# Adding a projection's output bias to the residual on GpSimd instead of as four matrix products

## The chip, the cores and the metric

The kernel runs on one core of one Trainium2 chip, as one program. The metric is the device time in microseconds (us) of one execution; of several runs the median counts, and lower is better. The core has five engines that run side by side, each with its own instruction stream: TensorE (PE in the rows, with PEld for its weight loads), VectorE (DVE), ScalarE (ACT), GpSimd (POOL) and SyncE (SP), which starts the weight transfers. They meet only at semaphores.

## The reference: what is computed

Two transformer-like blocks over 256 tokens of width 1024, in float32. The first block has a banded attention, a squared-ReLU MLP, a Griffin recurrent layer and a second MLP; the second block has a gated MLP, a mixing layer and another gated MLP. The change is about the last line of the recurrent layer and the residual that it is added to:

```python
def rglru_block(h, w_in, b_in, conv_w, conv_b, w_ga, b_ga, w_gx, b_gx, a_param, w_o, b_o):
    u = jnp.einsum('bsd,de->bse', h, w_in) + b_in
    ...            # convolution over 4 taps, two sigmoid gates, a scan over time
    out = hs.astype(h.dtype) * y_br
    return jnp.einsum('bse,ed->bsd', out, w_o) + b_o
...
        h = h + mix                       # mix is the rglru_block of rmsnorm(h)
        h = h + sq_relu_mlp(rmsnorm(h, norm_mlp[layer]), mlp_w1[layer], mlp_w2[layer])
```

`b_o` has 1024 numbers, one for each column of `h`, and is the same for all 256 tokens.

## The kernel before, in words

The residual `h` stays in SBUF as two tiles of 128 tokens by 1024 columns. All order is written by hand: each engine has one function (`sync`, `scalar`, `vector`, `gpsimd`, `tensor`) that issues its instructions in program order, and waits on semaphores where it needs another engine.

Every weight matrix comes in pieces of 128x2048 float32 (1 MB). A piece is split into two float32r parts, since one float32r product alone would be too coarse: ScalarE copies `raw` to `w_hi` (`hi(n)`, L386), VectorE writes `w_lo = raw - w_hi` (`lo(n)`, L784), and TensorE makes three products for each block (high by high, high by low, low by high). Pieces of 8 row blocks go through `u_piece` (`u_block`, L1456 to L1459), pieces of output projections through `d_piece` and `d_part` (L1493).

At each layer's start (`turn(j, ...)` on three engines) VectorE adds the accumulators to `h` (L805), TensorE transposes `h` (L1519), ScalarE and VectorE split it to `xT_hi` and `xT_lo` (L400, L813). The norm's row factors follow later and beside: VectorE makes `var` (L820), GpSimd raises it to the power -1/2 (`rstds(j)`, L1385), VectorE scales the identity by it (`diags(j)`, L828, two of 128x128), TensorE multiplies these with ones (`spread(j)`, L1561), and VectorE copies the result to `rms` (L851).

The recurrent layer is called L1 (`N_REC` is its first piece, `N_RO` the first piece of its output projection). TensorE goes through eight `u_piece`s. Between their blocks stand `spread(L1)` (in the second piece) and the small products `gates(n)` (L1764, L1765, from the third piece on). `gates(n)` waits for three convolution taps of VectorE (`conv(p)`, L1165), which need `x_pair(p)` (L1156), which needs `rms`. On VectorE the order after `var` is: `lo(N_REC + 2)`, the two `diags`, a small fill of the convolution's padding (L1199), `lo(N_REC + 3)`, the copy of `rms`, `x_pair(0)`, `conv(0)`. GpSimd has `rstds(L1)`, then four products `bx` (L1417) and four `squares` (L1423), all 128x512.

The bias: GpSimd's queue starts a transfer that lays `b_o` over all 128 partitions. During the first MLP ScalarE and VectorE split it into a high and a low part, one in even and one in odd rows (L595, L596, L1136 to L1145). Before the output projection, TensorE writes the bias into the four accumulators with four products that contract over two rows only (L1786), in four different row groups of the array; the projection's products add to that. The first of them, in `d_piece(N_RO)`, waits for `z_lo` (L1196), which VectorE finishes late.

Of the kernel before, what the change touches and what calls it, by code (L numbers as in the profile page):

```python
# [7 lines left out]
F32R = mybir.dt.float32r  # L8
BF16 = mybir.dt.bfloat16
ACT = mybir.ActivationFunctionType  # L10
ALU = mybir.AluOpType
# [94 lines left out]
def r32(ap):  # L106
    return ap.bitcast(F32)


def build(nc, A, out):  # L110
    def sb(name, shape, dt=F32):
        return nc.alloc_sbuf_tensor(name, shape, dt)[tuple(slice(None) for _ in shape)]
# [22 lines left out]
    tiny = sb("tiny", [P, 6, 4])  # L135
    sink = sb("sink", [P, HEADS_2])
    vbuf = sb("v", [P, T, D])
    b_o = sb("b_o", [P, D], F32R)
    both = sb("both", [P, P], F32R)
    firsts = sb("firsts", [P, 2])  # L140
    work_bytes = 47 * 1024
    work = nc.alloc_sbuf_tensor("work", [P, work_bytes // 4], F32)
    bank = [nc.alloc_psum_tensor(f"bank{i}", [P, 512], F32)[:, :] for i in range(8)]
# [2 lines left out]
    def at(kib, *shape):  # L146
        n, o = int(np.prod(shape)), int(kib * 256)
        assert (o + n) * 4 <= work_bytes, (kib, shape)
        v = work[:, o:o + n]
        if len(shape) == 1:  # L150
            return v
        names = "abcd"[:len(shape)]
        return v.rearrange(f"p ({' '.join(names)}) -> p {' '.join(names)}", **dict(zip(names, shape)))
# [8 lines left out]
    def vec(name, i=0):  # L162
# [42 lines left out]
        "bx_done"))  # L205
    a_done, sq_done, m_done, mult_done, b_done, hs_done, y_done, o_done = (sem(n) for n in (
        "a_done", "sq_done", "m_done", "mult_done", "b_done", "hs_done", "y_done", "o_done"))
    bo_hi, bo_rest, bo_done = sem("bo_hi"), sem("bo_rest"), sem("bo_done")

    mix_left, pc_closed, pc_left, pool_d, d_left, k_rot, v_turned, v2_done = (sem(n) for n in (  # L210
        "mix_left", "pc_closed", "pc_left", "pool_d", "d_left", "k_rot", "v_turned", "v2_done"))
# [67 lines left out]
            return pair(z_hi[:, p, :]), pair(z_lo[:, p, :])  # L279
        return blocks(xT_hi, p), blocks(xT_lo, p)  # L280

    bo_raw, bo_low = at(24, D), at(28, D)
    nf = at(8, D)

    q2, k2, v2 = at(24, 4, S), at(28, 4, S), vbuf[:, :, 0:P]
# [61 lines left out]
    def row_bcast(a, n, rows=P):  # L347
        return bass.AP(tensor=a.tensor, offset=a.offset, ap=[[0, rows], [1, n]])
# [32 lines left out]
    def scalar(e):  # L381
# [66 lines left out]
                e.wait_ge(hn_done, t + 1)  # L448
                e.activation(at(16 + 4 * t, D), h[:, t, :], ACT.Square, accum_out=ssq2[:, t:t + 1]).then_inc(hn_ss, 1)

        def feed_forward(f, beside=None):
            if f.nu == 2:
                low_leaves(f, 0, 0)
            if f.j != M1:
                hi(f.n0 + LOOK)
            if f.nu == 2:
                if f.j == F1:
                    normed_squares()
                low_leaves(f, 0, 1)
                hi(f.n0 + 1 + LOOK)  # L460
                gate(f, 0)
            z_finish(f, 0)
            if f.j == M1:
                hi(f.n0 + LOOK)
            for p in range(1, f.pairs):
                n = f.ups(p)
                if beside and p == 6:
                    beside()
                if n + LOOK < TOTAL:
                    hi(n + LOOK)  # L470
                if f.nu == 2:
                    gate(f, p)
                    if n + 1 + LOOK < TOTAL:
                        hi(n + 1 + LOOK)
                z_finish(f, p)
                if n + f.nu + LOOK < TOTAL:
                    hi(n + f.nu + LOOK)
# [112 lines left out]
        hi(N_WO + 2 + LOOK)  # L590
        split_o(a1, 3)

        def bias_hi():
            e.wait_ge(in_b_o, 16)
            e.activation(b_o, bo_raw, ACT.Copy).then_inc(bo_hi, 1)  # L595
            e.activation(both, ones[:, 0:P], ACT.Copy).then_inc(bo_hi, 1)  # L596

        turn(M0, N_WO + 3 + LOOK)
        feed_forward(FM0, bias_hi)


        turn(L1, N_REC - 1 + LOOK)
# [178 lines left out]
    def vector(e):  # L781
# [122 lines left out]
            e.wait_ge(hn_done, 2)  # L904
            e.tensor_tensor(rstd, rstd, rstd2, ALU.mult).then_inc(rstd_both, 1)

        def feed_forward(f, beside=None):
            if f.nu == 2:
                sums(f, 0, 0, tmp[0])
                if f.j == F1:  # L910
                    normed_h()
            if f.j != M1:
                lo(f.n0 + LOOK)
            if f.nu == 2:
                if f.j == F1:
                    normed_variance()
                sums(f, 0, 1, tmp[1])
                lo(f.n0 + 1 + LOOK)
                if f.j == F1:
                    both_rstds()  # L920
                    diags(F1)
            if f.nu == 1:

                e.wait_ge(var_done, f.j + 1)
                e.reciprocal(down_scale, var).then_inc(scale_done, 1)
            else:
                spread(f.j)
                e.tensor_scalar(down_scale, rstd, 0.5, None, ALU.mult).then_inc(scale_done, 1)
                gate(f, 0)
            z_finish(f, 0)  # L930
            if f.j == M1:
                lo(f.n0 + LOOK)
            for p in range(1, f.pairs):
                n = f.ups(p)
                if beside and p == 7:
                    beside()
                if n + LOOK < TOTAL:
                    lo(n + LOOK)
                if f.nu == 2:
                    gate(f, p)  # L940
                    if n + 1 + LOOK < TOTAL:
                        lo(n + 1 + LOOK)
                z_finish(f, p)
                if n + f.nu + LOOK < TOTAL and not (f.j == F1 and p == f.pairs - 1):
                    lo(n + f.nu + LOOK)
# [99 lines left out]
        def beside(a, j, first_waits=()):  # L1045

            if j > 1:
                copy_turned(a, j - 1)
            for hd in range(2):
                mask_and_max(a, j, hd)  # L1050
# [80 lines left out]
        split_o(a1, 3)  # L1131
        lo(N_WO + 2 + LOOK)

        def bias_split():

            e.tensor_tensor(firsts, ident[:, 0:2], ident[:, 32:34], ALU.add).then_inc(bo_rest, 1)  # L1136
            for i in (2, 3):
                e.wait_ge(bo_rest, i - 1)
                e.tensor_tensor(firsts, firsts, ident[:, 32 * i:32 * i + 2], ALU.add).then_inc(bo_rest, 1)
            e.wait_ge(bo_hi, 1)  # L1140
            e.tensor_tensor(bo_low, bo_raw, r32(b_o), ALU.subtract).then_inc(bo_rest, 1)
            e.wait_ge(bo_rest, 4)
            e.tensor_scalar(bo_low, bo_low, firsts[:, 1:2], None, ALU.mult).then_inc(bo_rest, 1)
            e.wait_ge(bo_rest, 5)
            e.scalar_tensor_tensor(out=b_o, in0=r32(b_o), scalar=firsts[:, 0:1], in1=bo_low, op0=ALU.mult,  # L1145
                                   op1=ALU.add).then_inc(bo_done, 1)

        turn(M0, FM0.n0)
        feed_forward(FM0, bias_split)


        turn(L1, N_REC)
# [94 lines left out]
        mixed_lo(3)  # L1247
        lo(FM1.n0)

        turn(M1, FM1.n0, 1)  # L1250
        lo(FM1.n0 + 2)
        feed_forward(FM1)
# [129 lines left out]
    def gpsimd(e):  # L1382
# [24 lines left out]
        e.dma_start(gate_w[:, 1], A["w_gx"].rearrange("n c e -> c n e")).then_inc(in_gate_x, 16)  # L1407
        e.dma_start(pool_w, A["pool_w"].rearrange("n c e -> c n e")).then_inc(in_pool_w, 16)
        e.dma_start(sink, row_bcast(A["sink"], HEADS_2)).then_inc(in_sink, 16)
        e.dma_start(bo_raw, row_bcast(A["b_o"], D)).then_inc(in_b_o, 16)  # L1410


        rstds(L1)

        def bx(p):
            e.wait_ge(ig_done, 2 * p + 2)
# [28 lines left out]
    def tensor(e):  # L1445
# [331 lines left out]
        u_piece(N_REC + 6, bank[7])  # L1777
        e.wait_ge(x_left, 4)
        u_piece(N_REC + 7, bank[4])
        e.wait_ge(bo_done, 1)  # L1780
        e.wait_ge(bo_hi, 2)
        e.wait_ge(ig_done, KB)
        for t in range(T):
            for half in range(2):
                r = slice(32 * (2 * t + half), 32 * (2 * t + half) + 2)
                e.matmul(acc[t][half], both[r, :], b_o[r, half * HALF:(half + 1) * HALF], start=True, stop=False,  # L1786
                         skip_group_check=True)
        for i in range(2):
            e.wait_ge(mix_lo, 4 + i + 1)
            d_piece(N_RO + i, from_z(i))  # L1790
        one, two = (N_RO + 2, from_z(2)), (N_RO + 3, from_xT(3))
        e.wait_ge(mix_lo, 4 + 3)
        split(N_RO + 2)
# [209 lines left out]
```

## Time and profile before

| | us |
|---|---|
| three runs | 1012.96, 1013.86, 1013.97 |
| median | 1013.86 |
| profiled execution, its own time | 1013.26 |
| its span, first to last instruction | 1011.5 |
| TensorE busy | 1003.2 (99%) |
| VectorE busy | 684.5 (68%) |
| ScalarE busy | 556.8 (55%) |
| GpSimd busy | 35.0 (3%) |

A row of the timeline gives the start in us from the span's start, the duration in us, the engine, the line of the kernel, the operation, its output and inputs, and in brackets how long the engine sat idle before it and who ended that. Records of two instructions in a row on one engine overlap by some hundredths of a us, since an instruction is started before the one ahead of it has fully drained.

### The profile page before, as it was taken

To read this page: it belongs to the slowest core of one execution; us is meant where nothing else is said; L and a number is where in the kernel's file an instruction comes from. 1 tells how busy PE (TensorE), PEld (TensorE's weight loads), DVE (VectorE), ACT (ScalarE), POOL (GpSimd) and SP (SyncE) were. 2 spreads that over 40 slices of the span, in tenths; PEclk is the share of its full clock that TensorE was granted. 3 is DMA by queue.
4 is the path that set the end of the run, shared out by engine and by line. 5 is a ranking of instruction groups with operands and counts; after the bars stand their busy time and mean duration, and the time that the engine had idled before them with its cause. 6 is when DMAs were issued, how large, how long until landed. Compare 5 with 4: busy or idle time off the path is not lost.

```text
span 1011.5 us, 14177 instructions
## 1 busy us (share of the span) xinstructions
PE 1003.2 (99%) x5632; PEld 857.4 (85%) x5632; DVE 684.5 (68%) x925; ACT 556.8 (55%) x807; POOL 35.0 (3%) x38
## 2 busy tenths in 40 slices
PE   9999999999999999999999999999999999999997
PEld 7988788888889988888888888888888788888886
DVE  6777676666667887666566766656578767666564
ACT  6678654444456866443444645545457655545453
POOL 1000010000002300000000200000010010000000
PEclk9999999999999999999999999999999999999999
DMA  9943385564553445745655566565633365665621
GB/s 339 324 133 126 125 280 176 200 208 167 188 187 126 167 167 193 245 167 199 212 173 171 207 198 226 190 208 167 208 114 107 115 204 172 228 208 167 208 84 42
DMA packets 122287, 185.13 MB, mean 183 GB/s; under 512 B 3130, under 2 KB 100590, under 8 KB 122094
## 3 DMA queue, kind: packets, MB, share of 16 engines
q1 hardware_dynamic: 119952, 176.70, 52.4%
q0 software_dynamic: 1808, 6.93, 1.9%
q8 instruction: 45, 0.74, 0.3%
q10 hardware_dynamic: 462, 0.60, 0.2%
q14 instruction: 20, 0.16, 0.0%
HBM read 183.14 MB, written 1.07 MB: 182 GB/s over the span
## 4 chain that ended last, share of the span: by engine, by line
PE 96%; DVE 2%; ACT 1%; DMA 1%; issue 1%; SPq 0%
PE bank L1493 37%; PE bank L1470 28%; PE bank L1472 14%; PE bank L1456 3%; PE bank L1458 3%; PE bank L1459 3%; PE bank L1519 1%; DVE w_lo L784 1%; PE bank L1614 1%; PE bank L1665 1%; PE bank L1642 1%; PE bank L1626 1%; DMA raw<-in_w_qkv 1%; PE bank L1810 0%; PE bank L1811 0%
## 5 line engine op out<-in xcount | busy, mean ns | idle before, releaser
L784 DVE TENSOR_TENSOR w_lo<-raw,w_hi 128x2048 fp32r<-128x2048 f32 x164 | 374.0, 2289 | 130.5 <-ACT w_hi L386 130.5
L1470 PE MATMUL bank<-xT,w_hi 128*128 128x512 f32 x1216 | 431.4, 398 | 0.0
L1472 PE MATMUL bank<-xT,w_lo 128*128 128x256 f32 x1216 | 341.1, 280 | 0.0
L386 ACT ACTIVATE w_hi<-raw 128x2048 fp32r<-128x2048 f32 x164 | 311.7, 1908 | 37.5 <-PE bank L1493 33.5
L1470 PEld LDWEIGHTS bank<-xT,w_hi 128*128 128x128 f32 x1216 | 228.4, 188 | 55.7 <-issue 0.3
L1472 PEld LDWEIGHTS bank<-xT,w_lo 128*128 128x128 f32 x1216 | 229.6, 189 | 1.9
L1493 PE MATMUL bank<-w_hi,z_hi 128*128 128x512 f32 x472 | 153.9, 394 | 0.2
L1493 PE MATMUL bank<-w_lo,z_hi 128*128 128x512 f32 x472 | 152.3, 391 | 0.0
L1493 PE MATMUL bank<-w_hi,z_lo 128*128 128x512 f32 x472 | 151.7, 390 | 0.0
L429 ACT ACTIVATE work<-bank 128x256 f32<-128x256 f32 x152 | 49.8, 379 | 178.8 <-PE bank L1472 178.8
L859 DVE TENSOR_TENSOR work<-bank,work 128x256 f32<-128x256 f32 x152 | 57.1, 418 | 74.0 <-ACT work L429 74.0
L1493 PEld LDWEIGHTS bank<-w_lo,z_hi 128*128 128x128 f32 x472 | 88.6, 188 | 19.3 <-issue 0.2
L1493 PEld LDWEIGHTS bank<-w_hi,z_lo 128*128 128x128 f32 x472 | 88.6, 188 | 19.3
L1493 PEld LDWEIGHTS bank<-w_hi,z_hi 128*128 128x128 f32 x472 | 85.0, 188 | 18.5 <-issue 1.3
L1456 PE MATMUL bank<-xT,w_hi 128*128 128x256 f32 x304 | 89.9, 296 | 0.0
L444 ACT ACTIVATE z_hi<-work 128x512 fp32r<-128x512 f32 x54 | 34.1, 632 | 99.7 <-DVE work L876 53.0
L1458 PE MATMUL bank<-xT,w_hi 128*128 128x256 f32 x304 | 85.9, 282 | 0.0
L1459 PE MATMUL bank<-xT,w_lo 128*128 128x256 f32 x304 | 85.8, 282 | 0.0
L887 DVE TENSOR_TENSOR z_lo<-work,z_hi 128x512 fp32r<-128x512 f32 x54 | 37.4, 692 | 37.7 <-ACT z_hi L444 37.7
L1456 PEld LDWEIGHTS bank<-xT,w_hi 128*128 128x128 f32 x304 | 58.0, 191 | 2.4 <-issue 1.2
L1458 PEld LDWEIGHTS bank<-xT,w_hi 128*128 128x128 f32 x304 | 58.1, 191 | 0.3
L1459 PEld LDWEIGHTS bank<-xT,w_lo 128*128 128x128 f32 x304 | 58.1, 191 | 0.0
(215 smaller groups left out, 775.5 us busy)
## 6 DMA issues: line engine op xcount, KB each, us to landing
raw<-in_w SPq DMA_DIRECT2D x64, 1024.0 KB, 5.3
raw<-in_f_gate SPq DMA_DIRECT2D x22, 1024.0 KB, 5.3
raw<-in_f_up SPq DMA_DIRECT2D x22, 1024.0 KB, 5.8
raw<-in_f_down SPq DMA_DIRECT2D x22, 1024.0 KB, 4.9
raw<-in_w_in SPq DMA_DIRECT2D x13, 1024.0 KB, 5.4
raw<-in_w_qkv SPq DMA_DIRECT2D x9, 1024.0 KB, 8.6
raw<-in_w_o SPq DMA_DIRECT2D x4, 1024.0 KB, 5.0
raw<-in_rec_w_o SPq DMA_DIRECT2D x4, 1024.0 KB, 5.2
```

What stands on the lines that cost most here:

```text
L386: e.activation(w_hi[n % RING], raw[n % RAW], ACT.Copy).then_inc(hi_done, 1)
L429: e.activation(low[:, b * S:(b + 1) * S], bank[n][:, S:2 * S], ACT.Copy).then_inc(z_low, 1)
L444: e.activation(z_hi[:, s, :], tmp[f.nu], ACT.Copy).then_inc(zhi_done, 1)
L784: e.tensor_tensor(w_lo[n % RING], raw[n % RAW], r32(w_hi[n % RING]), ALU.subtract).then_inc(lo_done, 1)
L859: e.tensor_tensor(t[:, here], bank[n][:, 0:S], low[:, here], ALU.add).then_inc(z_sum, 1)
L887: e.tensor_tensor(z_lo[:, s, :], z, r32(z_hi[:, s, :]), ALU.subtract).then_inc(zlo_done, 1)
L1456: e.matmul(o, whi[:, k, cut], xT_hi[:, k, :], start=(k == 0 and b == 0), stop=False, skip_group_check=True)
L1458: e.matmul(o, whi[:, k, cut], xT_lo[:, k, :], start=False, stop=False, skip_group_check=True)
L1459: last = e.matmul(o, wlo[:, k, cut], xT_hi[:, k, :], start=False, stop=(k == KB - 1), skip_group_check=True)
L1470: e.matmul(bank[i], whi[:, k, cut], xT[:, k, :, :].rearrange("p b s -> p (b s)"), start=(k == 0), stop=False, skip_group_check=True)
L1472: last = e.matmul(bank[i][:, 0:S], wlo[:, k, cut], xT_hi[:, k, :], start=False, stop=(k == KB - 1), skip_group_check=True)
L1493: mm = e.matmul(acc[t][half], x, w[:, kk, half * 512:(half + 1) * 512], start=(first and kk == 0 and x is xhi and w is whi), stop=(last an ...
```

## The change

The four products are gone, and so is all that prepared them: ScalarE's two copies and VectorE's six instructions in the first MLP, and the tiles `both` and `firsts`. `b_o` is now plain float32, loaded by the same transfer. GpSimd adds it to the two tiles of `h`, with two instructions of 128x1024, straight behind `rstds(L1)`, once TensorE has transposed `h` for this layer. VectorE waits for both additions before it next adds to `h` (`turn(M1, ...)`). The first product of the output projection now starts its accumulators (`first`) in place of the bias products.

```diff
-    b_o = sb("b_o", [P, D], F32R)
-    both = sb("both", [P, P], F32R)
-    firsts = sb("firsts", [P, 2])
+    b_o = sb("b_o", [P, D])
...
-        def bias_hi():
-            e.wait_ge(in_b_o, 16)
-            e.activation(b_o, bo_raw, ACT.Copy).then_inc(bo_hi, 1)
-            e.activation(both, ones[:, 0:P], ACT.Copy).then_inc(bo_hi, 1)
...
-        def bias_split():
...
-            e.wait_ge(bo_hi, 1)
-            e.tensor_tensor(bo_low, bo_raw, r32(b_o), ALU.subtract).then_inc(bo_rest, 1)
...
+        e.wait_ge(bo_done, T)
         turn(M1, FM1.n0, 1)
...
         rstds(L1)
+
+        e.wait_ge(in_b_o, 16)
+        e.wait_ge(turned, KB * L1 + KB)
+        for t in range(T):
+            e.tensor_tensor(h[:, t, :], h[:, t, :], b_o, ALU.add).then_inc(bo_done, 1)
...
-        e.wait_ge(bo_done, 1)
-        e.wait_ge(bo_hi, 2)
         e.wait_ge(ig_done, KB)
-        for t in range(T):
-            for half in range(2):
-                r = slice(32 * (2 * t + half), 32 * (2 * t + half) + 2)
-                e.matmul(acc[t][half], both[r, :], b_o[r, half * HALF:(half + 1) * HALF], start=True, stop=False,
-                         skip_group_check=True)
         for i in range(2):
             e.wait_ge(mix_lo, 4 + i + 1)
-            d_piece(N_RO + i, from_z(i))
+            d_piece(N_RO + i, from_z(i), first=(i == 0))
```

GpSimd's queue in the changed program, from the last small transfer of the first MLP to the recurrent layer's squares (line numbers are those of the changed kernel; `work` holds `xc`, `ig`, `rr` and others):

```order
L1384 DMA sink<-in_sink 128x8
L1385 DMA b_o<-in_b_o 128x1024
L1360 TENSOR_TENSOR rstd<-var,minus_half 128x2 [waits var_done]
L1393 TENSOR_TENSOR h<-h,b_o 128x1024 [waits turned,in_b_o]
L1393 TENSOR_TENSOR h<-h,b_o 128x1024
L1397 TENSOR_TENSOR work<-work 128x512 [waits ig_done] x4
L1403 TENSOR_TENSOR work<-work 128x512 [waits a_done] x2
```

Before, the four `bx` stood right behind `rstd`; now the two additions stand between them.

TensorE's queue before, at the border from the last `u_piece` to the output projection:

```order
L1458 MATMUL bank<-xT,w_hi 128x256
L1459 MATMUL bank<-xT,w_lo 128x256
L1786 MATMUL bank<-b_o,both 128x512 [waits ig_done,bo_hi,bo_done]
L1786 MATMUL bank<-b_o,both 128x512 x3
L1493 MATMUL bank<-w_hi,z_hi 128x512 [waits lo_done,hi_done,mix_lo]
L1493 MATMUL bank<-w_hi,z_hi 128x512
```

The same place in the changed program:

```order
L1438 MATMUL bank<-xT,w_hi 128x256
L1439 MATMUL bank<-xT,w_lo 128x256
L1473 MATMUL bank<-w_hi,z_hi 128x512 [waits hi_done,lo_done,mix_lo,ig_done]
L1473 MATMUL bank<-w_hi,z_hi 128x512
L1473 MATMUL bank<-w_lo,z_hi 128x512 x2
```

The projection's first product now follows the last `u_piece` directly and takes over the wait for `ig_done`.

## Rows read from the trace of the kernel before

**Rows 1.** The page, parts 1, 2 and 4: busy time, granted clock, ending chain.

```profile
PE 1003.2 (99%) x5632; PEld 857.4 (85%) x5632; DVE 684.5 (68%) x925; ACT 556.8 (55%) x807; POOL 35.0 (3%) x38
...
PEclk9999999999999999999999999999999999999999
...
PE 96%; DVE 2%; ACT 1%; DMA 1%; issue 1%; SPq 0%
```

**Rows 2.** Waits of TensorE's products: engine, line, releaser, total us, times, longest.

```profile
PE bank L1650 <- POOL zeros L1387: 1.0, 1, 1.0
PE bank L1626 <- DVE work L990: 0.9, 2, 0.5
PE bank L1665 <- ACT w_hi L391: 0.2, 1, 0.2
```

**Rows 3.** Timeline, VectorE and GpSimd, at the start of the recurrent layer.

```profile
306.22 2.28 DVE L784 TENSOR_TENSOR w_lo<-raw,w_hi 128x2048 fp32r<-128x2048 f32 x1
306.40 2.69 POOL L1385 TENSOR_TENSOR rstd<-var,minus_half 128x2 f32<-128x2 f32 x1 [175.31 <-DVE var L820]
...
309.12 0.28 DVE L828 TENSOR_SCALAR diag<-ident,rstd 128x128 f32<-128x128 f32 x1 [0.61 <-POOL rstd L1385]
309.32 0.28 DVE L828 TENSOR_SCALAR diag<-ident,rstd 128x128 f32<-128x128 f32 x1
309.60 2.28 DVE L784 TENSOR_TENSOR w_lo<-raw,w_hi 128x2048 fp32r<-128x2048 f32 x1
312.17 0.42 DVE L851 COPY rms<-bank 128x256 f32<-128x256 f32 x1 [0.29 <-PE bank L1561]
...
314.05 0.48 DVE L1165 SCALAR_TENSOR_TENSOR work<-work,cols 128x256 f32<-128x256 f32 x1 [0.73 <-ACT work L619]
315.09 0.48 DVE L1165 SCALAR_TENSOR_TENSOR work<-work,cols 128x256 f32<-128x256 f32 x1
```

**Rows 4.** Timeline, TensorE's weight loads of `spread(L1)` and of `gates(0)`.

```profile
311.40 0.19 PEld L1561 LDWEIGHTS bank<-diag,ones 128*128 128x128 f32 x1
...
316.16 0.19 PEld L1764 LDWEIGHTS bank<-work,gate_w 128*128 128x128 f32 x1
```

**Rows 5.** Timeline, GpSimd's `bx` beside VectorE.

```profile
321.22 2.28 DVE L784 TENSOR_TENSOR w_lo<-raw,w_hi 128x2048 fp32r<-128x2048 f32 x1
322.16 2.50 POOL L1417 TENSOR_TENSOR work<-work 128x512 f32<-128x512 f32 x1 [13.07 <-ACT work L610]
...
325.12 1.30 POOL L1417 TENSOR_TENSOR work<-work 128x512 f32<-128x512 f32 x1 [0.47 <-ACT work L610]
325.97 0.74 DVE L1165 SCALAR_TENSOR_TENSOR work<-work,cols 128x256 f32<-128x256 f32 x1 [1.86 <-ACT work L619]
```

**Rows 6.** Timeline, GpSimd's `squares` beside VectorE.

```profile
344.46 1.04 POOL L1423 TENSOR_TENSOR work<-work 128x512 f32<-128x512 f32 x1 [2.26 <-ACT work L625]
345.46 1.04 POOL L1423 TENSOR_TENSOR work<-work 128x512 f32<-128x512 f32 x1
345.54 1.51 DVE L1176 SCALAR_TENSOR_TENSOR work<-work 128x512 f32<-128x512 f32 x1 [1.05 <-POOL work L1423]
346.97 0.68 DVE L1176 SCALAR_TENSOR_TENSOR work<-work 128x512 f32<-128x512 f32 x1
```

**Rows 7.** One tile's or line's instructions: duration in ns, min/median/max.

```profile
L784 DVE TENSOR_TENSOR w_lo<-raw,w_hi x164: 2272/2292/2295, 19.6 to 985.6; 128x2048 fp32r<-128x2048 f32 x164
...
L1141 DVE TENSOR_TENSOR work<-work,b_o x1: 1220/1220/1220, 197.5 to 197.5; 128x1024 f32<-128x1024 f32 x1
...
L1143 DVE TENSOR_SCALAR work<-work,firsts x1: 754/754/754, 198.7 to 198.7; 128x1024 f32<-128x1024 f32 x1
```

**Rows 8.** Timeline, the border before the output projection.

```profile
355.78 0.69 DVE L1196 TENSOR_TENSOR z_lo<-work,z_hi 128x512 fp32r<-128x512 f32 x1
...
356.07 0.28 PE L1459 MATMUL bank<-xT,w_lo 128*128 128x256 f32 x1
356.27 0.51 PE L1786 MATMUL bank<-b_o,both 2*128 2x512 f32 x4
356.71 0.73 PE L1493 MATMUL bank<-w_hi,z_hi 128*128 128x512 f32 x2
357.28 0.63 PE L1493 MATMUL bank<-w_lo,z_hi 128*128 128x512 f32 x2
```

**Rows 9.** Timeline, TensorE, a like border in the first MLP.

```profile
190.02 0.28 PE L1472 MATMUL bank<-xT,w_lo 128*128 128x256 f32 x1
190.13 0.63 PE L1493 MATMUL bank<-w_hi,z_hi 128*128 128x512 f32 x2
190.60 0.62 PE L1493 MATMUL bank<-w_lo,z_hi 128*128 128x512 f32 x2
```

More of the change, by code:

```diff
@@ L207, in build @@
         "a_done", "sq_done", "m_done", "mult_done", "b_done", "hs_done", "y_done", "o_done"))
-    bo_hi, bo_rest, bo_done = sem("bo_hi"), sem("bo_rest"), sem("bo_done")
+    bo_done = sem("bo_done")
     mix_left, pc_closed, pc_left, pool_d, d_left, k_rot, v_turned, v2_done = (sem(n) for n in (
@@ L280, in rec_home @@
         return blocks(xT_hi, p), blocks(xT_lo, p)
-    bo_raw, bo_low = at(24, D), at(28, D)
     nf = at(8, D)
@@ L449, in normed_squares, with feed_forward @@
                 e.activation(at(16 + 4 * t, D), h[:, t, :], ACT.Square, accum_out=ssq2[:, t:t + 1]).then_inc(hn_ss, 1)
-        def feed_forward(f, beside=None):
+        def feed_forward(f):
             if f.nu == 2:
@@ L466, in feed_forward @@
                 n = f.ups(p)
-                if beside and p == 6:
-                    beside()
                 if n + LOOK < TOTAL:
@@ L591, in scalar @@
         split_o(a1, 3)
-        def bias_hi():
-            e.wait_ge(in_b_o, 16)
-            e.activation(b_o, bo_raw, ACT.Copy).then_inc(bo_hi, 1)
-            e.activation(both, ones[:, 0:P], ACT.Copy).then_inc(bo_hi, 1)
         turn(M0, N_WO + 3 + LOOK)
-        feed_forward(FM0, bias_hi)
+        feed_forward(FM0)
         turn(L1, N_REC - 1 + LOOK)
@@ L905, in both_rstds, with feed_forward @@
             e.tensor_tensor(rstd, rstd, rstd2, ALU.mult).then_inc(rstd_both, 1)
-        def feed_forward(f, beside=None):
+        def feed_forward(f):
             if f.nu == 2:
@@ L934, in feed_forward @@
                 n = f.ups(p)
-                if beside and p == 7:
-                    beside()
                 if n + LOOK < TOTAL:
@@ L1132, in vector @@
         lo(N_WO + 2 + LOOK)
-        def bias_split():
[L1136 to L1139, printed above, removed]
-            e.wait_ge(bo_hi, 1)
-            e.tensor_tensor(bo_low, bo_raw, r32(b_o), ALU.subtract).then_inc(bo_rest, 1)
[L1142 to L1146, printed above, removed]
         turn(M0, FM0.n0)
-        feed_forward(FM0, bias_split)
+        feed_forward(FM0)
         turn(L1, N_REC)
@@ L1409, in gpsimd @@
         e.dma_start(sink, row_bcast(A["sink"], HEADS_2)).then_inc(in_sink, 16)
-        e.dma_start(bo_raw, row_bcast(A["b_o"], D)).then_inc(in_b_o, 16)
+        e.dma_start(b_o, row_bcast(A["b_o"], D)).then_inc(in_b_o, 16)
         rstds(L1)
+        e.wait_ge(in_b_o, 16)
+        e.wait_ge(turned, KB * L1 + KB)
+        for t in range(T):
+            e.tensor_tensor(h[:, t, :], h[:, t, :], b_o, ALU.add).then_inc(bo_done, 1)
         def bx(p):
```

## The prediction

> **What bounds the kernel now.** I read the page first: TensorE is busy for 1003.2 of 1011.5 us, and the chain that ended last lies on it for 96% [rows 1]. Then the waits: in the whole program TensorE's products wait for another engine only four times by name, 2.1 us together, the longest 1.0 [rows 2]. So there is one bound, TensorE, from end to end. Two things follow. Work taken from another engine is worth nothing. And work put on another engine costs nothing until it makes TensorE wait; from there on it costs all of it, because nothing behind gives it back. The question is thus how much slack TensorE's suppliers have where the additions now stand. The timeline of that place is [rows 3, 4].
>
> **What is taken away.** ScalarE's two copies and VectorE's six instructions in the first MLP (the two widest shown, 1.22 and 0.75 us, in [rows 7]) lie beside a TensorE that waits for neither: 0 us. The DMA of the bias is the same one as before.
>
> The four products start together at 356.27, in four row groups, and the projection's first product starts at 356.71 [rows 8]. At the like border in the first MLP the next product starts 0.11 us behind the last one of the piece (190.02 to 190.13) and the second pair 0.47 us behind the first [rows 9]; here the second pair is 0.57 behind (356.71 to 357.28), 0.10 more. So if nothing else held the projection, it could start at 356.07 + 0.12 = 356.19, and the gain would be 0.52 + 0.10 = 0.62 us. But something else holds it: `z_lo` ends at 355.78 + 0.69 = 356.47. The waiting engine resumes some 0.04 behind such an end (309.09 to 309.12, or 345.50 to 345.54), so at 356.51: the gain is 0.20 + 0.10 = 0.30. The products stood mostly in a gap that TensorE has to wait through anyway. Bounds 0 and 0.62; I take 0.25.
>
> **What is added.** Two additions of 128x1024 on GpSimd. No row has one. The nearest is `bx`, also two different inputs and in place, at 128x512: 1.30 us when it starts free, and 1.16 us from the end of VectorE's L784 (321.22 + 2.28 = 323.50) to its own end (324.66) when it had been waiting [rows 5]. A wide one is one start and twice the work: 1.30 + 1.16 = 2.46. Bounds: a `square`, which reads one tensor twice, takes 1.04 [rows 6], twice that is 2.08; twice 1.30 is 2.60. I take 2.45 each, 4.9 together.
>
> **Where they stand, and what they do to VectorE.** These rows say that GpSimd and VectorE exclude each other for whole instructions, when VectorE reads two tensors of SBUF. In [rows 5] `bx` starts at 322.16 inside L784 and takes 2.50 instead of 1.30. In [rows 6] VectorE's L1176 comes at 345.54, when the second square has just begun at 345.46, and takes 1.51 where its successor takes 0.68; it ends 0.55 behind the square's end at 346.50. The 128x2 power of `rstd` itself takes 2.69, up to 0.59 behind the end of the L784 beside it (308.50) [rows 3]. Whoever is first runs, and the other stands. L784 was never the second so far: 164 of them within 2272 to 2295 ns [rows 7]. Now it will be.
>
> The Trainium skill says this as a rule ("SBUF — State Buffer", section "Who interferes with whom"): the port pair is a lock held for the full instruction, and a VectorE `tensor_scalar` in its two-port mode takes it too. The first half agrees with the three rows above. The second would put `diags` among the blocked, which no row of before shows. By it the sum is the one with blocked `diags` (+3.5), read without it the other (+3.1).
>
> For `diags` the row that bears is L1143: a TENSOR_SCALAR of 128x1024 in 0.75 us, where L1141, with two tensors, takes 1.22 [rows 7]. It moves two elements at a time, so it may well use both ports; I take it as blocked, and give the sum without it below.
>
> Now in order of time. `rstd` ends at 309.09. GpSimd starts its next instruction 0.04 ahead of the end of a record (345.46 against 345.50) [rows 6], VectorE 0.03 behind it, at 309.12 [rows 3]. So addition 1 comes first: 309.05 to 311.50. Addition 2 starts at 311.46, to 313.91. `diags` have stood since 309.12: the first ends at about 313.91 + 0.15, the second 0.20 later, at 314.26 (if the first slips in between the additions, the second still ends there). `lo(N_REC + 3)` follows, 2.28, to 316.54, instead of 311.88. The copy of `rms`, now at 312.17, starts at 316.46, since in a full queue the next starts up to 0.08 ahead (309.32 against 309.12 + 0.28). From there to the end of the third tap is 315.57 - 312.17 = 3.40 [rows 3], so `gates(0)` can load at 319.86 + 0.04 = 319.90, instead of 316.16 [rows 4]. Its slack now is 316.16 - 315.61 = 0.55; VectorE's delay is 4.29; TensorE loses **3.74 us**. About 2.7 of it appears already at `spread(L1)`, which comes at 311.40 and waits for the `diags`.
>
> Nothing is gained back: `gates(1)` and later ones move with TensorE, and VectorE's next conv must wait for ScalarE behind later gates anyway (1.86 us idle at 325.97, [rows 5]), so the delay doesn't grow either. Queued behind the additions on GpSimd is `bx(0)`, which starts only at 322.16: free. VectorE's new wait for both additions comes some 60 us after them: free.
>
> **Sum:** +3.74 - 0.25 = +3.5 us. The profiled execution took 1013.26, the median of the runs is 1013.86, 0.6 above it; I count from the median: **1017.4 us** (a profiled one near 1016.8). With additions of 2.08 the two save 0.75: +2.75, with 2.60 it is +3.8. If `diags` aren't blocked, they end at 309.60 as now, `lo(N_REC + 3)` waits to 313.91 and ends near 316.1: +3.1. This case alone reaches from 1016.4 to 1017.9.
>
> The Trainium skill has a price for such an addition ("GPSIMD Engine Reference", section "Elementwise — side-by-side cycle accounting"): 4497 ns at 2048 elements. Half of it, an estimate, is 2.25 us, and the sum would be 0.4 lower; no run here shows it yet.
>
> **The rivals.**
> - *VectorE gets in between the additions with all it has waiting.* `diags` at 311.5 to 311.9, `lo(N_REC + 3)` to 314.2, addition 2 from 314.05 (0.15 ahead of that record's end, as `bx` was, 1.16 instead of 1.30 us, in [rows 5]) to 316.5. The first tap would come at 316.0 and stands to 316.5, the third ends near 317.8: 2.25 late, less 0.55 slack, 1.7 us; less 0.25, **+1.45, 1015.3**. For it: a waiting VectorE is ready when addition 1 ends. Against: GpSimd's next is issued before the end of the last, and between two `diags` the port is free for a moment. Not slower by what can be told. It decides from the point on which addition 2 begins before or behind L784. Chance 0.22.
> - *The additions hide wholly*, GpSimd giving way to VectorE each time or the wide addition being shorter than I think; only the four products are left of the change: -0.3, down to -0.62, **1013.6**. For it: `bx` gave way at 322.16 and nobody lost. Against: there L784 had been first; and GpSimd is the one that stands ready at 309.05. Chance 0.12.
> - *TensorE's clock falls.* It is at its full level in all 40 slices [rows 1], and TensorE's longest wait is 1.0 us [rows 2]. Now it stands 2.7 us in one stretch. Each us that it then runs at 1.2 instead of 2.4 GHz costs half a us; three of them make **1018.9**. Chance 0.05.
>
> **How the numbers follow.** The forecast has 0.61, the rivals 0.22, 0.12 and 0.05. About 0.2% (2.0 us) is what a measurement of this kernel can tell from no change. The forecast is beyond it for all its bounds (+2.5 to +4.0), with the last rival that makes 0.66 slower; the first two rivals are within it, 0.32; 0.02 is left for faster, since all that TensorE is rid of is 0.62 us. The range must take in the first rival, and leaves out the hidden case and the clock: 1014.9 to 1018.1; the forecast's own is 1016.4 to 1017.9.
>
> **What the profile would show.** Two additions of about 2.45 us on GpSimd from 309.05; a `diag` of over 2 us in place of 0.28 (about 4.9 if both additions come first); TensorE's weight load of `spread(L1)` behind a wait of about 2.7 us for it, that of `gates(0)` behind another of about 1; the projection's first product held by `z_lo`. I'd be wrong if addition 2 is found behind L784, if `diags` keep 0.28, or if the additions take under 1.8 us.

## The result and the profile after

The changed kernel takes 1016.99 us in the median of eight runs (1016.62 to 1017.68), the kernel before 1013.77 (1012.96 to 1014.73): **3.2 us slower, ratio 1.0034, 95% interval 1.0023 to 1.0044**. I had forecast 1017.4 us, 3.5 above a median of 1013.86.

The page of the changed kernel, its parts 1 and 2, answers to [rows 1]. TensorE's busy time is the same within 0.9 us, the span is 3.6 longer, and one of its 40 slices has dropped from 9 tenths to 8, the one from about 305 us on:

```profile
span 1015.1 us, 14165 instructions
...
PE 1004.1 (99%) x5628; PEld 857.6 (84%) x5628; DVE 685.6 (68%) x919; ACT 556.3 (55%) x805; POOL 39.6 (4%) x40
...
PE   9999999999998999999999999999999999999997
```

The last of these lines in the page of the kernel before:

```profile
PE   9999999999999999999999999999999999999997
```

Waits of TensorE's products (engine, line, releaser, total us, times, longest), against [rows 2]; L1541 is `spread(L1)`, L1744 `gates(n)`, and both stood in no list of before:

```profile
PE bank L1541 <- DVE diag L818: 1.8, 1, 1.8
...
PE bank L1744 <- DVE work L1139: 0.8, 1, 0.8
```

The timeline of GpSimd and VectorE at the start of the recurrent layer, against [rows 3]. This execution's rows lie 0.33 us later from the start on (`rstd` 306.73, before 306.40), so subtract 0.33 to compare:

```profile
306.73 2.69 POOL L1360 TENSOR_TENSOR rstd<-var,minus_half 128x2 f32<-128x2 f32 x1 [175.31 <-DVE var L810]
309.39 2.41 POOL L1393 TENSOR_TENSOR h<-h,b_o 128x1024 f32<-128x1024 f32 x1
309.44 2.44 DVE L818 TENSOR_SCALAR diag<-ident,rstd 128x128 f32<-128x128 f32 x1 [0.61 <-POOL rstd L1360]
311.77 2.33 POOL L1393 TENSOR_TENSOR h<-h,b_o 128x1024 f32<-128x1024 f32 x1
311.80 2.38 DVE L818 TENSOR_SCALAR diag<-ident,rstd 128x128 f32<-128x128 f32 x1
314.19 2.28 DVE L774 TENSOR_TENSOR w_lo<-raw,w_hi 128x2048 fp32r<-128x2048 f32 x1
316.39 0.41 DVE L841 COPY rms<-bank 128x256 f32<-128x256 f32 x1
318.26 2.96 DVE L1139 SCALAR_TENSOR_TENSOR work<-work,cols 128x256 f32<-128x256 f32 x6 [0.73 <-ACT work L609]
```

The reader is to see one pair of rows twice: an addition, and a `diag` that starts 0.05 us (then 0.03) behind it and ends 0.08 behind its end. A `diag` of 0.28 us took 2.4: it stood until GpSimd's addition was through. ("The port", below, is what the prediction calls the port pair of SBUF, which one of the two engines holds while the other stands; so these two don't meet only at semaphores, as the first section has it.) Everything behind on VectorE's queue is late: L774 by 4.26 us (314.19 - 0.33 against 309.60), the first tap by 3.88 (318.26 - 0.33 against 314.05).

TensorE's weight loads at the two waits, against [rows 4]:

```profile
311.94 0.30 PEld L1541 LDWEIGHTS bank<-diag,ones 128*128 128x128 f32 x2
314.24 0.30 PEld L1541 LDWEIGHTS bank<-diag,ones 128*128 128x128 f32 x2 [2.01 <-DVE diag L818]
...
319.84 0.30 PEld L1744 LDWEIGHTS bank<-work,gate_w 128*128 128x128 f32 x2 [1.00 <-DVE work L1139]
```

And the border to the output projection, against [rows 8]:

```profile
359.46 0.69 DVE L1170 TENSOR_TENSOR z_lo<-work,z_hi 128x512 fp32r<-128x512 f32 x1
...
359.74 0.28 PE L1439 MATMUL bank<-xT,w_lo 128*128 128x256 f32 x1
360.25 0.70 PE L1473 MATMUL bank<-w_hi,z_hi 128*128 128x512 f32 x2 [0.24 <-issue]
360.79 0.62 PE L1473 MATMUL bank<-w_lo,z_hi 128*128 128x512 f32 x2
```

The products are gone, but the projection still begins 0.51 us behind the last product of the piece (before 0.64), 0.10 behind the end of `z_lo` at 360.15. From the last product to the second pair it is 1.05 us now and was 1.21: 0.16 gained.

### The profile page after: what moved, and what is told of

Read it like the earlier page. It is cut to its first block, busy times and chain, and to the rows that moved or that the text cites. A ratio compares the mean times of both kernels' runs of the same rounds, so it can differ in the third digit from the quotient of the medians.

```text
span 1015.1 us, 14165 instructions
## 1 busy us (share of the span) xinstructions
PE 1004.1 (99%) x5628; PEld 857.6 (84%) x5628; DVE 685.6 (68%) x919; ACT 556.3 (55%) x805; POOL 39.6 (4%) x40
## 4 chain that ended last, share of the span: by engine, by line
PE 76%; issue 18%; DVE 3%; ACT 1%; POOL 1%; DMA 1%; SPq 0%; ACTq 0%; POOLq 0%
PE bank L1473 28%; PE bank L1450 22%; PE bank L1452 11%; PE bank L1436 3%; PE bank L1439 3%; PE bank L1438 3%; DVE w_lo L774 1%; PE bank L1594 1%; PE bank L1645 1%; PE bank L1499 1%; PE bank L1622 1%; PE bank L1606 1%; DMA raw<-in_w_qkv 1%; DVE diag L818 0%; PE bank L1783 0%
## 5 line engine op out<-in xcount | busy, mean ns | idle before, releaser
L774 DVE TENSOR_TENSOR w_lo<-raw,w_hi 128x2048 fp32r<-128x2048 f32 x164 | 374.1, 2289 | 131.9 <-ACT w_hi L383 131.8
```

Of the source, the lines that this page charges most:

```text
L774: e.tensor_tensor(w_lo[n % RING], raw[n % RAW], r32(w_hi[n % RING]), ALU.subtract).then_inc(lo_done, 1)
```

## The experiments

Whole-program times carry some tenths of noise, so the table gives the stage itself too: distances in us from the start of the record of `rstd` in this layer, each the difference of two starts in the profiled execution. "gates(0)" is its first product, "last u" the last product of the eight pieces, "projection" its first product, "next layer" the first transposition for the MLP behind.

| kernel | median (runs) | ratio, 95% interval | gates(0) | last u | projection | next layer |
|---|---|---|---|---|---|---|
| before | | | 9.88 | 49.67 | 50.32 | 69.52 |
| the change | 1016.99 (8) | 1.0034 [1.0023, 1.0044] | 13.12 | 53.01 | 53.53 | 72.68 |
| e1_no_bias | 1013.43 (11) | 0.9998 [0.9989, 1.0007] | 9.89 | 49.67 | 50.19 | 69.34 |
| e2_scratch_adds | 1017.62 (5) | 1.0038 [1.0025, 1.005] | 13.63 | 53.42 | 54.06 | 73.26 |
| e3_one_add | 1014.92 (11) | 1.0011 [1.0002, 1.002] | 11.01 | 50.90 | 51.41 | 70.56 |
| e4_behind_diags | 1015.42 (11) | 1.0019 [1.001, 1.0028] | 11.50 | 51.40 | 51.90 | 71.07 |
| e5_dve_gaps | 1014.15 (11) | 1.0005 [0.9996, 1.0014] | 9.88 | 49.81 | 50.77 | 69.94 |
| e6_gpsimd_gaps | 1017.81 (5) | 1.0038 [1.0024, 1.0051] | 9.88 | 49.67 | 52.85 | 72.00 |
| e7_dve_four_waits | 1013.67 (11) | 0.9999 [0.999, 1.0008] | 9.88 | 49.67 | 50.18 | 69.31 |
| e8_dve_and_reorder | 1013.74 (11) | 0.9999 [0.999, 1.0008] | 9.88 | 49.67 | 49.79 | 69.37 |
| e9_before_reorder | 1013.67 (11) | 0.9998 [0.999, 1.0007] | 9.88 | 49.67 | 50.32 | 69.52 |
| e10_four_adds | 1016.53 (8) | 1.0026 [1.0016, 1.0036] | 12.06 | 53.57 | 54.08 | 73.21 |
| e11_change_again | 1016.91 (1) | | 13.64 | 53.43 | 53.95 | 73.11 |
| e12_change_again | 1017.81 (1) | | 13.64 | 53.43 | 53.95 | 73.11 |

The kernel before had medians of 1013.54 beside e1 to e4, 1013.49 beside e5 and e6, 1013.81 beside e7 to e10, and 1013.67 beside e11 and e12.

The prediction counts `gates(0)` by its first weight load. On the scale of the table that is at 9.76 before, 13.12 in the change, 11.01 in e3, 12.06 in e10, 13.52 in e11 and 13.53 in e12: where TensorE didn't wait, the product starts 0.12 behind its load, where it waited, with it. So the change loses 3.36 us there by the load and 3.24 by the product; the last product of the pieces comes 3.34 late.

**The two halves of the change apart.** First the removal alone:

```diff
-        e.wait_ge(in_b_o, 16)
-        e.wait_ge(turned, KB * L1 + KB)
-        for t in range(T):
-            e.tensor_tensor(h[:, t, :], h[:, t, :], b_o, ALU.add).then_inc(bo_done, 1)
...
-        e.wait_ge(bo_done, T)
```

> The changed kernel without the two additions and without VectorE's wait for them; the bias of the output projection is left out of the result. What is left of the change is only that the four products, and their preparation, are gone. My theory: TensorE starts the output projection when z_lo is ready, so 0.15 to 0.3 us are gained against the kernel before (1013.77), and the waits of 2.0 us at spread(L1) and 1.0 us at gates(0) are gone. Rival (the products were worth their whole 0.62 us, and the additions cost 3.8): 0.6 us faster than before.

No measurable gain in time (the interval reaches from 0.9989 to 1.0007); in the trace the stage is 0.18 us shorter (69.34 against 69.52), and the waits of the change are gone (`gates(0)` at 9.89). So the products were worth 0.18 in the stage, not 0.62, and the whole loss is the additions'.

Then the additions alone, on data that nobody needs, with the products kept:

```diff
         rstds(L1)
+        for t in range(T):
+            e.tensor_tensor(vbuf[:, t, :], vbuf[:, t, :], h[:, t, :], ALU.add).then_inc(scratch, 1)
```

> The kernel before, with its four products kept, and with two additions of 128x1024 on GpSimd at the same place that read h and write to a tile that nobody needs then. My theory: the loss comes from GpSimd holding VectorE off, whatever it computes: diag takes about 2.4 us twice, TensorE loses 3.3 to 3.5 us, so +3.4 us against before, 0.15 to 0.3 more than the change itself. Rival (the loss comes from adding in place to h, or from the projection's first product starting the accumulators): no change against before.

3.8 per mille, 4.1 us slower, the same two places. What the additions compute plays no part; that GpSimd runs then does. The stage is 3.74 us longer (73.26), more than the change's 3.16 by 0.58. The change's own execution with a fallen clock (e11, below) has 73.11: so 0.15 are the products, and 0.43 is the clock.

**One addition, and a later start.**

```diff
-        for t in range(T):
+        for t in range(1):
             e.tensor_tensor(h[:, t, :], h[:, t, :], b_o, ALU.add).then_inc(bo_done, 1)
```

> The changed kernel with only the first of the two additions; the bias is left out for the second 128 tokens. My theory: the first diag stands 2.4 us, the second follows 0.2 us behind it, lo(N_REC + 3) ends 2.2 us later than before, the first 0.37 us of it vanish in VectorE's wait for spread(L1), 0.55 in the slack of gates(0): TensorE loses 1.25 us, less 0.2 for the products: +1.1 us against before. Rival (loss proportional to GpSimd's time): half of the change's, +1.6 us.

Measured +1.4 us by the medians, and +1.04 in the stage (70.56 against 69.52); `gates(0)` comes 1.13 late, its weight load 1.25, as expected. Half the GpSimd time costs a third of the loss, because the first 0.9 us (VectorE's wait for `spread(L1)` and the slack of `gates(0)`) are free once. The rival that counts GpSimd's time predicts 1.6. The times alone don't exclude it (their interval reaches from 0.2 to 2.0 us); the stage speaks against it.

```diff
         e.wait_ge(turned, KB * L1 + KB)
+        e.wait_ge(diag_done, 2 * SPREAD[L1])
         for t in range(T):
```

> The changed kernel, with GpSimd waiting for both diags before it adds. The semaphore comes some 0.04 us after lo(N_REC + 3) has started on VectorE, so this one goes first. My theory: addition 1 stands behind it and runs from 2.1 to 4.5 us after the diags; no wait at spread(L1); the copy of rms and x_pair(0), which read one tensor of SBUF at most, run beside it unhindered; the first tap slips in between the additions, the second stands until addition 2 has ended: taps end 1.75 us late, less 0.55 slack, less 0.2: +1.0 us. Rival (no slipping in, both additions ahead of the first tap): +1.6 us. Rival (copy and x_pair are held too): +3 us or more.

Measured +1.9 us by the medians, +1.55 in the stage: my 1.0 was wrong, the rival "no slipping in" (1.6) was right. (The profiled execution took 1017.25; it also waits 1.6 us for a `w_lo` in the program's first 30 us, ahead of this stage.) The timeline of that kernel:

```profile
312.12 2.29 DVE L774 TENSOR_TENSOR w_lo<-raw,w_hi 128x2048 fp32r<-128x2048 f32 x1
314.70 0.42 DVE L841 COPY rms<-bank 128x256 f32<-128x256 f32 x1 [0.29 <-PE bank L1542]
315.16 0.69 DVE L1130 TENSOR_TENSOR work<-bank,rms 128x512 f32<-128x512 f32 x1
316.58 2.75 DVE L1139 SCALAR_TENSOR_TENSOR work<-work,cols 128x256 f32<-128x256 f32 x1 [0.73 <-ACT work L609]
...
312.30 4.37 POOL L1394 TENSOR_TENSOR h<-h,b_o 128x1024 f32<-128x1024 f32 x1 [0.69 <-DVE diag L818]
316.63 2.42 POOL L1394 TENSOR_TENSOR h<-h,b_o 128x1024 f32<-128x1024 f32 x1
```

Addition 1 came second this time and waited for L774. The copy and L1130, with at most one input in SBUF, ran beside it at full speed (0.42 and 0.69, as before), so of the VectorE instructions seen here only those with two SBUF inputs, and the `diag` kind, were held. The first tap came at 316.58, only 0.09 ahead of the end of addition 1's record (316.67): too late, addition 2 had the port, and the tap ended 0.28 behind it, as in [rows 5]. In the changed kernel the first `diag`, which had stood there since 309.44, got in at the same kind of border. My reading was: coming 0.09 us before a record's end isn't enough, waiting well before it is.

**Smaller pieces.** That reading can be tested: with four additions, what waits at each border should get in.

```diff
         for t in range(T):
-            e.tensor_tensor(h[:, t, :], h[:, t, :], b_o, ALU.add).then_inc(bo_done, 1)
+            for half in range(2):
+                here = slice(half * HALF, (half + 1) * HALF)
+                e.tensor_tensor(h[:, t, here], h[:, t, here], b_o[:, here], ALU.add).then_inc(bo_done, 1)
```

> The changed kernel with the same additions on GpSimd at the same place, but as four of 128x512 instead of two of 128x1024. My theory: at the end of each GpSimd instruction a VectorE instruction that already waits gets in. So the first diag goes behind addition 1, the second behind addition 2, lo(N_REC + 3) behind addition 3, and addition 4 runs beside the copy of rms and x_pair(0), which it doesn't hold. The lo then ends 3.4 to 3.6 us late instead of 4.2, or 1.2 us earlier than in the changed kernel: the loss shrinks from 3.2 us to about 2.0. Rival (only the sum of GpSimd's work counts, or GpSimd keeps the port between its instructions): 3.2 us or more slower than before, as the change, plus some tenths for two more starts.

```profile
309.41 7.18 POOL L1395 TENSOR_TENSOR h<-h,b_o 128x512 f32<-128x512 f32 x4
...
309.47 2.58 DVE L818 TENSOR_SCALAR diag<-ident,rstd 128x128 f32<-128x128 f32 x2 [0.61 <-POOL rstd L1360]
311.98 1.27 DVE L1173 TENSOR_SCALAR work<-cols 128x24 f32<-128x24 f32 x1
313.16 2.28 DVE L774 TENSOR_TENSOR w_lo<-raw,w_hi 128x2048 fp32r<-128x2048 f32 x1
```

At the first two borders one VectorE instruction got in, a `diag` each time. At the third it was two: the padding L1173, whose place in the queue I had forgotten (0.17 us became 1.27), and right behind it L774, ahead of addition 4, which waits:

```profile
311.94 1.27 POOL L1395 TENSOR_TENSOR h<-h,b_o 128x512 f32<-128x512 f32 x1
313.18 3.42 POOL L1395 TENSOR_TENSOR h<-h,b_o 128x512 f32<-128x512 f32 x1
```

L774 started at 313.16, only 0.05 before the end of addition 3's record (313.21) and 0.02 before addition 4's start, and went first; the second `diag`, which came 0.04 behind the start of addition 2 (310.72 against 310.68), stood. So my reading of e4_behind_diags, by the distance from the record's end, doesn't hold as a rule: its tap came earlier than this L774 and stood. What decides such a close race stays open. The four additions took 7.18 us, the two wide ones 4.71. `gates(0)` comes 2.18 late instead of 3.24, where 2.0 had been expected. This shows that what has stood through an addition gets in at its end, and refutes that GpSimd keeps the port between its instructions. Yet the median is 2.7 us slower, since the stage then loses 1.6 more between `gates(0)` and the last product (53.57 - 12.06 = 41.51, in the change 53.01 - 13.12 = 39.89). That is the clock:

```profile
318.00:322.00 4.00, 3.19 (x11) 2.83 (x12) 3.16 (x7) 2.58 (x4) 0.00 (x0) 0.61 0.55 194
322.00:326.00 4.00, 4.00 (x28) 3.76 (x28) 3.86 (x7) 3.64 (x7) 0.67 (x1) 0.96 0.00 0
```

In the first row (busy time of PE, PEld, DVE, ACT, POOL with their counts, then the granted clock, DMA share, GB/s) TensorE was granted 0.61 of its clock: it ran partly at 1.2 GHz, directly behind a wait of 2.1 us. What the two rows lack of a full clock, 0.39 and 0.04 of 4 us, is 1.7 us, about what the stage loses. The eight executions of this kernel fall in two groups, 1015.02 to 1015.77 (mean clock 0.998 to 0.999) and 1017.29 to 1017.80 (0.996 to 0.997), 2 us apart. The profile is of the upper group; that the lower one kept its clock is argued from the means, not shown.

**The change again, for its clock.** No edit.

> The changed kernel once more, one profiled execution. Its eight runs lie between 1016.62 and 1017.68 us, with a mean granted clock of 0.997 to 0.999, and in e2_scratch_adds and e10_four_adds TensorE was granted 0.70 and 0.61 of its full clock in the stretch behind its wait. My theory: the engine waits are the same as in the first profile (diag about 2.4 us twice, TensorE's waits 2.0 and 1.0), and only whether the clock falls behind them differs from execution to execution, which would explain the upper runs: span 1015.1 with full clock, 1015.6 to 1016 with a stretch at half. Rival (the handover of the port between GpSimd and VectorE varies): other durations of the diags.

> As e11_change_again, a third profiled execution of the changed kernel. Theory: the same durations of the diags and the same two waits of TensorE, whatever the clock does. Rival: durations of the diags that differ.

In both, VectorE's pair of `diags` took 4.74 and 4.75 us (4.75 the first time), so the handover is the same each time. The clock is not: 0.59 in the first of these and 0.73 in the second, in the stretch behind `spread(L1)`, where the first profile of the change had 1.00.

```profile
314.00:318.00 4.00, 3.99 (x21) 3.99 (x22) 3.26 (x4) 0.61 (x2) 0.00 (x0) 0.59 0.16 25
```

But the wait for `gates(0)` has gone from TensorE's list in both: at half clock it arrives there late, where it would have waited 1.0 us anyway. It costs 0.42 us by the last product of the pieces (53.43 against 53.01; the weight load of `gates(0)` comes 0.40 later), not 1.6. e2_scratch_adds had the same: 0.70 in that stretch, `gates(0)` at 13.63. But the fall doesn't explain which executions are long, as I had expected: e11 has the span of the first profile, 1015.1 us, with a fallen clock. e12 has 1016.0, and 0.77 of the 0.9 between the two lies ahead of this stage (`rstd` starts at 307.26 and 306.49).

**The additions where the engines have room.** If the loss is a matter of place, another place should be free. First VectorE in place of GpSimd, four pieces of 128x512: two ahead of `conv(2)`, one ahead of `conv(3)`, one ahead of `mults(0)`.

```diff
+        def bias_half(t, half):
+            here = slice(half * HALF, (half + 1) * HALF)
+            e.tensor_tensor(h[:, t, here], h[:, t, here], b_o[:, here], ALU.add).then_inc(bo_done, 1)
...
+        bias_half(0, 0)
+        bias_half(0, 1)
         conv(2)
...
+        bias_half(1, 0)
         conv(3)
...
+        bias_half(1, 1)
         mults(0)
```

> The bias is added to h by VectorE instead of GpSimd, in four pieces of 128x512 (0.69 us each by the width of its other two-tensor instructions), placed where VectorE stood idle before: two ahead of conv(2) (idle 1.86 us), one ahead of conv(3) (1.43), one ahead of the first mults (1.05). GpSimd does no additions. My theory: all four are hidden, no waits at spread(L1) and gates(0), and only the gain of the products is left: 0.2 us faster than before, 3.4 faster than the change. Rival (VectorE has no room, the chain to z_lo is pushed back): 0.5 to 2 us slower than before.

No waits at `spread(L1)` and `gates(0)`, but not the gain I expected: 0.42 us lost in the stage. The last piece met GpSimd's squares:

```profile
345.42 2.49 POOL L1409 TENSOR_TENSOR work<-work 128x512 f32<-128x512 f32 x2 [2.02 <-ACT work L615]
...
345.48 1.53 DVE L1135 TENSOR_TENSOR h<-h,b_o 128x512 f32<-128x512 f32 x1
346.93 2.12 DVE L1154 SCALAR_TENSOR_TENSOR work<-work 128x512 f32<-128x512 f32 x2
```

The piece waited through the first square and pushed back the second (2.49 for two, before 1.04 each, 2.04 together), and the chain of squares, mults, scans and `z_lo` is the one that the projection waits for. The 1.05 us in which VectorE had been idle there were a wait of that chain, not room. The two pieces ahead of `conv(2)` weren't free either: the weight load of `gates(2)` comes 0.14 us later than before, and so does the last product of the pieces (49.81).

With one piece ahead of each conv instead, where VectorE waited for ScalarE:

```diff
         x_pair(0)
+        bias_half(0)
         conv(0)
...
         x_pair(1)
+        bias_half(1)
         conv(1)
...
         x_pair(2)
+        bias_half(2)
         conv(2)
...
         x_pair(3)
+        bias_half(3)
         conv(3)
```

> As the run with VectorE's four pieces, but one piece ahead of each of the four convs, where VectorE waited for ScalarE 0.73, 0.73, 1.86 and 1.43 us before and where GpSimd holds the port at most for a bx. My theory (the 0.7 us that the earlier run lost came from its last piece, which got between two squares of GpSimd, delayed the mults and so z_lo): no wait at gates and spread, the projection's first product at most 0.1 us later behind the last one of the piece than in the changed kernel; time as the kernel before, -0.3 to +0.1 us. Rival (a piece of 0.69 in a gap of 0.73 costs more than it shows, since the slack of gates(0) is 0.55): +0.5 us.

As expected: `gates(0)` at 9.88, the stage 0.21 us shorter than before (69.31), the time that of the kernel before (ratio 0.9999) and 3.3 us below the change by the medians. The same arithmetic on the same `h`, in 0.7 us gaps:

```profile
313.34 0.69 DVE L1130 TENSOR_TENSOR work<-bank,rms 128x512 f32<-128x512 f32 x1
313.94 0.68 DVE L1136 TENSOR_TENSOR h<-h,b_o 128x512 f32<-128x512 f32 x1
314.76 2.96 DVE L1144 SCALAR_TENSOR_TENSOR work<-work,cols 128x256 f32<-128x256 f32 x6
```

Then GpSimd's own wide additions, but later:

```diff
         for p in range(4):
+            if p >= 2:
+                e.wait_ge(conv_tap, 6 * (p + 1))
+                e.tensor_tensor(h[:, p - 2, :], h[:, p - 2, :], b_o, ALU.add).then_inc(bo_done, 1)
             bx(p)
```

> The same two additions of 128x1024 on GpSimd, but later: the first behind conv(2), ahead of bx(2), the second behind conv(3), ahead of bx(3). At both places VectorE has lo pieces ahead or under way that TensorE needs only several us later. My theory: nothing at spread(L1) and gates(0); the first addition stands behind an L784 and delays bx(2) by 1 to 2 us, harmless; the second collides with the lo pieces ahead of y_pair(0), of which VectorE can take back the 0.55 and 1.05 us it idled: between 0.2 us faster and 0.8 us slower than before. Rival (GpSimd's additions cost VectorE their 4.7 us wherever they stand): 3 us slower than before.

Outside what I had expected: no wait at the start, but the projection starts 3.18 us behind the last product of the pieces, and the stage is 2.48 longer.

```profile
337.33 6.71 DVE L774 TENSOR_TENSOR w_lo<-raw,w_hi 128x2048 fp32r<-128x2048 f32 x2
...
337.49 4.40 POOL L1406 TENSOR_TENSOR h<-h,b_o 128x1024 f32<-128x1024 f32 x1 [2.32 <-DVE work L1139]
341.86 3.35 POOL L1393 TENSOR_TENSOR work<-work 128x512 f32<-128x512 f32 x1
345.17 4.08 POOL L1399 TENSOR_TENSOR work<-work 128x512 f32<-128x512 f32 x2
```

Here GpSimd and VectorE take turns: addition 2 waits for the first L774 and gets in ahead of the second (6.71 us for two, instead of 4.48), the last `bx` waits for the second and ends at 345.21, the squares behind it take 4.08, since the first of them waits for a third L774. I had counted VectorE's side and forgotten that GpSimd's own queue feeds the chain to `z_lo`. Its five executions spread from 1015.81 to 1019.74 at mean clocks of 0.995 to 0.999; why the upper ones are longer is open. The profiled one, the fastest, kept a granted clock of 1.00 behind this wait of 3.1 us; one fall as in e10_four_adds (1.6 us) would not cover the 3.9 us of the longest.

**What covers the four products.** VectorE makes `mixed(0)` and `mixed_lo(0)` earlier, once without and once with the products:

```diff
         inflow(1)
+        mixed(0)
         scan(2)
         scan(3)
-        mixed(0)
-        mixed(1)
         mixed_lo(0)
+        mixed(1)
```

> As e7_dve_four_waits, and VectorE makes mixed(0) ahead of the scans of the second pair and mixed_lo(0) ahead of mixed(1). My theory: z_lo for the projection's first piece ends 0.4 to 0.5 us earlier against the last product of the piece, TensorE no longer waits for it, and now the four products' removal shows: first product of the projection 0.11 us behind the last one of the piece instead of 0.51: 0.4 us faster than e7_dve_four_waits, 0.4 to 0.6 faster than before. Rival (another wait, for instance of the second piece's z_lo, takes the place at once): same as e7_dve_four_waits.

> The kernel before, its four products kept, with the same reorder of mixed(0) and mixed_lo(0) alone. My theory: z_lo is earlier, but the four products occupy TensorE until 356.7 in any case, so the projection starts at the same distance behind the piece's last product (0.64 us) or a tenth earlier: 0 to 0.1 us faster than before. Rival (z_lo alone set that start, the products are free of any cost): 0.4 us faster.

With the products kept, `z_lo` ends 0.39 us earlier and the projection starts at 50.32 as before: there the products set its start. Without them it starts at 49.79, only 0.12 behind the last product. So both things hold that start: `z_lo` (ended 50.08) allows it at 50.18, the products at 50.32, and taking away one leaves the other. But the 0.39 us don't reach the end of the layer: the next one begins at 69.37, no earlier than in e7_dve_four_waits (69.31). A new wait has come in:

```profile
PEld bank L1480 <- DVE xT L1175: 0.5, 1, 0.5
```

It is that for the projection's fourth input, made by the same VectorE queue. The rival of that run was right.

## Why the prediction was right, step by step

- **One bound, and slack to measure.** Right. The stage accounts for the loss: 3.16 us to the next layer in the first profile, 3.22 in the medians. That these are so near is in part luck, since two further profiles have 3.59 in the stage, with the clock's fall. Nothing was given back behind it.
- **The removed work is worth 0.25 us.** Right in cause, a little high: 0.18 in e1_no_bias, 0.21 in e7_dve_four_waits, by the stage; the whole times can't tell it from nothing. TensorE resumed 0.10 behind `z_lo`, where I had 0.04. ScalarE's and VectorE's removed instructions in the first MLP gave nothing that the times could show (ratio 0.9998, interval 0.9989 to 1.0007 in e1). The upper bound of 0.62 would have needed `z_lo` out of the way and VectorE's next inputs too (e8).
- **An addition takes 2.45 us.** 2.41 and 2.33; why the second is shorter isn't shown (in e4_behind_diags it took 2.42). The figure of the Trainium skill ("GPSIMD Engine Reference", "Elementwise — side-by-side cycle accounting") in the prediction gave an estimate of 2.25; the rows are between it and mine.
- **GpSimd first, `diags` blocked.** Right, and shown by their 2.44 and 2.38 us. The rule of the Trainium skill that a `tensor_scalar` in two-port mode is locked out too ("SBUF — State Buffer", "Who interferes with whom") agrees with this trace. It holds for the 128x24 one as well (1.27 us in e10_four_adds).
- **Both additions ahead of `lo(N_REC + 3)`.** Right. In detail the first `diag` got in between, a case I had named as ending at the same time; it ended 0.27 us earlier, since only the second `diag` was left, 0.08 behind the addition instead of 0.35. With the 0.14 of the additions' length L774 starts 0.40 earlier than I had it (313.86 against 314.26, on the time scale of before).
- **TensorE loses 3.74 us.** By the weight load of `gates(0)` it loses 3.36 with a full clock and 3.76 with a fallen one. The 0.40 that are missing with a full clock are those of L774 above: the third tap comes 3.89 late where I had 4.29, less 0.55 of slack. The split is 2.0 and 1.0 in the waits named, where I had 2.7 and about 1: the first half of `spread(L1)` needs only the first `diag`.
- **Rivals.** VectorE getting in with everything: between the two wide additions only the first `diag` got in; e10_four_adds shows how it goes with more borders. Additions hidden wholly: refuted there (e2), true for another place and engine (e7). The clock: real, in both repeated profiles of the change, but worth 0.4 us and not 1.5, since most of what it takes TensorE would have waited. I had put it at 0.05 and as an alternative to the forecast, where it is a part of it.

## What to carry to other kernels

GpSimd being idle 97% of the time is no licence: ask which VectorE instructions with two SBUF inputs, or in the faster `tensor_scalar` form, stand beside the new one and how much slack their readers have; here 0.55 us of slack stood against 4.7 us of lock. A wait of one engine is room for more work only if the chain it waits in doesn't pass through that same engine or its port: one piece in each gap behind a ScalarE step was free (e7), even where it took 1.17 us beside a `bx`; two in one gap cost 0.14 us (e5), and a gap in a chain through GpSimd was not free (e5, e6). And an operation that stands in the shadow of another wait is worth nothing to remove until that wait is gone, and then the next one has to be looked for (e8).

## What the runs showed of the hardware

- At the end of a GpSimd instruction, a VectorE instruction that has stood through it gets the port, even with GpSimd's next one ready, and the other way round: `diag` between two additions (2.44 and 2.38 us), an addition between two L774 (6.71 us for the pair). For one that comes just before the end it went either way: 0.09 us before it a tap stood (2.75 us, e4), 0.05 us before it an L774 behind a waiting instruction went first (2.28 us, e10).
- A `tensor_scalar` of 128x24 that takes 0.17 us alone takes 1.27 behind the lock.
- TensorE's clock fell to its lower level, 1.2 GHz, behind waits of 2.0 and 2.1 us, in e2, e10, e11 and e12. It did not in the first profile of the change with the same wait of 2.0, nor behind 1.7 us in e4 and 3.1 us in e6, so the length of the wait alone doesn't tell. At full load behind it the fall cost 1.6 us (e10), ahead of another wait 0.4 (e11).
